# Products and sums of the modulation vectors on GpSimd, interleaved in pairs, with the column as a per-partition scalar

## What is computed

```python
def adaln(cond, mod_w, mod_b):
    m = jax.nn.silu(cond) @ mod_w + mod_b        # mod_w: 1024 x 6144, one per layer
    return jnp.split(m, 6, axis=-1)

x = first_block(x, ...)                          # two layers, does not use m
...
sh1, sc1, g1, sh2, sc2, g2 = adaln(c, mod_w[i], mod_b[i])          # i = 0, 1
csh1, csc1, ... = adaln(c_ctx, mod_w[i], mod_b[i])                 # layer 0 only
a = rms_norm_2(h_lat, norm1_g[i]) * (1 + sc1) + sh1
```

## Time and profile before

| | before |
|---|---|
| median of three runs | 1936.33 us |
| profiled execution, span | 1938.2 us |
| PE busy | 1887.5 us (97%) |
| DVE busy | 784.5 us (40%) |
| ACT busy | 546.1 us (28%) |
| POOL busy | 734.9 us (38%), nearly all of it before 990 us |
| mean granted TensorE clock | 0.996 |

### The profile page before, as it was taken

How to read it: one execution, slowest core, us unless ns; L and a number is a source line. 1 busy time by engine, 2 the same in 40 slices (tenths; PEclk the granted TensorE clock), 3 DMA queues, 4 the chain that set the end, 5 groups by cost and what they waited for, 6 DMA issues and landing times.

```text
span 1938.2 us, 26187 instructions
## 1 busy us (share of the span) xinstructions
PE 1887.5 (97%) x9836; PEld 1008.9 (52%) x9836; DVE 784.5 (40%) x1672; ACT 546.1 (28%) x1187; POOL 734.9 (38%) x1065
## 2 busy tenths in 40 slices
PE   9999999999999999999999999999999999998998
PEld 6544556566546555565655456664543444444433
DVE  1445453433220344453346463753542411234533
ACT  3133433122421234421225231651311221012110
POOL 1767667765766667667630012100110100001111
PEclk9999999999999999999999999999999999999999
DMA  7323343334335243342332422313799822056997
GB/s 293 118 90 112 122 141 120 114 139 149 140 114 188 106 164 128 117 155 99 137 135 90 171 82 87 120 52 166 263 388 382 309 98 87 5 212 236 371 371 278
DMA packets 70300, 322.17 MB, mean 166 GB/s; under 512 B 8680, under 2 KB 11174, under 8 KB 55590
## 3 DMA queue, kind: packets, MB, share of 16 engines
q1 hardware_dynamic: 41688, 216.22, 29.7%
q0 software_dynamic: 25328, 92.81, 14.0%
q10 hardware_dynamic: 3168, 11.54, 1.5%
HBM read 287.51 MB, written 33.03 MB: 165 GB/s over the span
## 4 chain that ended last, share of the span: by engine, by line
PE 85%; DVE 5%; DMA 5%; issue 2%; ACT 1%; DVEq 1%; SPq 0%; POOL 0%; ACTq 0%; POOLq 0%
PE psA L462 23%; PE psA L1854 10%; PE psA L454 9%; PE psA L2001 6%; PE psA L1895 6%; PE psA L627 6%; PE psSO L2020 4%; PE psT L441 3%; PE psA L503 3%; PE psSO L532 3%; DMA pool_mem<-in_w_v 2%; PE psSO L542 2%; DMA pool_mem<-in_w_gu 1%; DVE pool_mem L2951 1%; PE psT L1970 1%
## 5 line engine op out<-in xcount | busy, mean ns | idle before, releaser
L462 PE MATMUL psA<-gB,pool_mem 128*128 128x512 f32 x1024 | 455.3, 597 | 0.0
L397 POOL TENSOR_TENSOR pool_mem<-pool_mem,cs 128x256 f32<-128x256 f32 x448 | 272.8, 641 | 136.0 <-DMA pool_mem<-in_mod_w 135.4
L462 PEld LDWEIGHTS psA<-gB,pool_mem 128*128 128x128 f32 x1024 | 189.5, 190 | 224.2 <-issue 224.2
L401 POOL TENSOR_TENSOR pool_mem<-pool_mem 128x256 f32<-128x256 f32 x336 | 248.1, 766 | 34.6 <-issue 26.6
L1854 PE MATMUL psA<-pool_mem 128*128 128x512 f32 (+1 forms) x528 | 209.0, 554 | 1.9 <-DVE pool_mem L1615 1.1
L454 PE MATMUL psA<-pool_mem,gB 128*128 128x256 f32 (+2 forms) x768 | 189.8, 403 | 2.7 <-ACT gB L796 1.2
L1803 POOL DMA_INDIRECT pool_mem<-xs_scratch,idx x38 | 35.5, 935 | 387.9 <-DVE idx L2625 359.5
L454 PEld LDWEIGHTS psA<-pool_mem,gB 128*128 128x128 f32 x768 | 143.8, 190 | 45.4 <-issue 6.2
L1854 PEld LDWEIGHTS psA<-pool_mem 128*128 128x128 f32 x528 | 99.2, 190 | 105.1 <-issue 99.8
L2001 PE MATMUL psA<-pool_mem 128*32 128x512 f32 (+1 forms) x896 | 141.1, 593 | 0.0
L1895 PE MATMUL psA<-pool_mem 128*128 128x512 f32 x256 | 113.9, 595 | 0.8 <-issue 0.8
(11 more groups left out here) (357 smaller groups left out, 2412.3 us busy)
## 6 DMA issues: line engine op xcount, KB each, us to landing
pool_mem<-in_w_gu SPq DMA_DIRECT2D x32, 2048.0 KB, 9.2
pool_mem<-in_mod_w POOLq DMA_DIRECT2D x56, 1024.0 KB, 7.9
pool_mem<-in_w_dn SPq DMA_DIRECT2D x32, 1024.0 KB, 13.8
pool_mem<-in_w_qk SPq DMA_DIRECT2D x24, 1024.0 KB, 4.9
ys_scratch<-pool_mem ACTq DMA_DIRECT2D x22, 512.0 KB, 10.1
pool_mem<-in_odd_w_in SPq DMA_DIRECT2D x5, 2048.0 KB, 9.7
pool_mem<-in_w_out SPq DMA_DIRECT2D x4, 2048.0 KB, 8.1
macc_scratch<-pool_mem POOLq DMA_DIRECT2D x56, 128.0 KB, 2.1
```

The lines of the kernel that those rows point to most:

```text
L397: nc.gpsimd.tensor_tensor(wm[:, b, k], wm[:, b, k], c_all[:, k].to_broadcast([P, MCH]), ALU.mult)
L401: nc.gpsimd.tensor_tensor(wm[:, b, k], wm[:, b, k], wm[:, b, n + k], ALU.add)
L462: m = nc.tensor.matmul(psA[:, n % 2, :], w(i), src[:, k, :], start=(i == 0), stop=(i == len(ks) - 1))
```

## The change

The 8 products, 7 sums and their operands stay the same in number. Seven of the eight products read the column of `cs` as a per-partition scalar instead of as a broadcast tensor; the product of slice 0 keeps the old form. The order is now: two products (slices k and 4 + k), a drain, their sum, a drain, four times; then the two sums, a drain, the last sum, a drain. A call of `multiply` has 10 drains instead of 4. Loads, stores, waits and all other engines are untouched.

```diff
             def multiply(b, row, loaded):
                 pool.wait_ge(m_loaded[b], loaded)
-                c_all = cs[:, row * KD:(row + 1) * KD].rearrange("p (k o) -> p k o", o=1)
-                for k in range(KD):
-                    nc.gpsimd.tensor_tensor(wm[:, b, k], wm[:, b, k], c_all[:, k].to_broadcast([P, MCH]), ALU.mult)
+                def times(k):
+                    if k == 0:
+                        c_0 = cs[:, row * KD:row * KD + 1]
+                        nc.gpsimd.tensor_tensor(wm[:, b, 0], wm[:, b, 0], c_0.to_broadcast([P, MCH]), ALU.mult)
+                        return
+                    nc.gpsimd.tensor_scalar(wm[:, b, k], wm[:, b, k], cs[:, row * KD + k:row * KD + k + 1], None, ALU.mult)
+
+                def plus(k, n, out):
+                    nc.gpsimd.tensor_tensor(out, wm[:, b, k], wm[:, b, n + k], ALU.add)
+
+                for k in range(4):
+                    times(k)
+                    times(4 + k)
+                    pool.drain()
+                    plus(k, 4, wm[:, b, k])
+                    pool.drain()
+                for k in range(2):
+                    plus(k, 2, wm[:, b, k])
                 pool.drain()
-                for n in (4, 2):
-                    for k in range(n):
-                        nc.gpsimd.tensor_tensor(wm[:, b, k], wm[:, b, k], wm[:, b, n + k], ALU.add)
-                    pool.drain()
-                nc.gpsimd.tensor_tensor(macc[:, b], wm[:, b, 0], wm[:, b, 1], ALU.add)
+                plus(0, 1, macc[:, b])
                 pool.drain()
```

## The result

The changed kernel takes 2137.84 us (median of 5 runs, 2135.53 to 2141.04) against 1936.33 us (5 runs, 1931.9 to 1937.83): a ratio of 1.1057, 95% interval 1.1031 to 1.1083. It is 201.5 us slower, where 1930.0 us and at the most 1953 us were predicted. The profiled execution spans 2136.3 us, 198.1 us more than the one before.

What follows compares the result with a forecast made beforehand. TensorE, busy 97% of the span, was taken to bound the kernel. From the 1938.2 us span, 7.2 us of removed blocks gave 1931.0 us; the run offset made it 1930.0 us, range 1926 to 1953 us, likeliest case 1926 to 1934.

Steps and rivals of the forecast that it cites:

- The two ways: GpSimd can move the time only through TensorE's few idle microseconds or by missing a date on which someone waits.
- the date: When SP, waiting for GpSimd's last store, must load the sums for DVE's `fold_columns`: 1029.9 us, about 40 us of slack.
- The runs are broken: GpSimd runs of at most two instructions end four full DVE blocks; 7.2 us gained, bounds 3.9 and 8.7 us.
- The 1.5 us set aside for smaller blocks: Allowance for DVE additions still held briefly: 0.7 us in the stretch of L1046, 0.8 us at two later places.
- Rival C: DVE blocks last one GpSimd instruction or return in small pieces elsewhere: 1936 us, between 1933 and 1939; chance 0.24.
- its last step: Result of the sum: 1931.0 us from the profiled span, 1929.1 us if all runs measure 1.9 us less; 1930.0 us taken.
- Seven products take a scalar: A GpSimd product by a per-partition scalar takes 0.40 us at 256 columns, range 0.29 to 0.61 us.
- Six more drains: Gaps in a GpSimd call: four of 0.24 us (or 0.42) before sums, five of 0.15 us between sums.
- The sum of a call: A `multiply` call takes 10.0 us, no change; with 0.1 us allowed, +6 us over 56 calls, GpSimd ending near 995 us.
- What the slack allows: With TensorE 7 us earlier, 33 us or 0.59 us a call; date missed from a scalar product of 0.48 us on.
- Rival B: GpSimd late at DVE's `fold_columns` wait, from scalar products over 0.48 us or larger gaps: 1946 to 1977 us; chance 0.24.

Runs made afterwards that it cites:

- shifted: Kernel before the change, with one memset and one product ahead of GpSimd's first load, runs of eight products unbroken: 1936.0 us, ratio 1.001.
- the two split kernels: Kernel before the change, drains added inside the second buffer's products: one after the fourth, 1929.89 us (0.9977); or after the third and sixth, 1928.14 us (0.9978).
- before_again: Kernel before the change, unchanged, profiled a second time: 1930.15 us (1 run), span 1928.6 us.
- sum_drains: Kernel before the change, with a drain after each of the six sums, four more drains per call: 1936.37 us (1 run).
- order_only: Changed kernel with its new order and ten drains, but all eight products in the old broadcast form: 2014.51 us, ratio 1.0408 to the kernel before.

## Why the prediction was wrong, step by step

**What bounds the kernel: right.** The two ways were named, and the time went through both: 14.5 us gained in the small gaps and behind them, 209.1 us lost at the date.

**The runs are broken: the mechanism right, one price left out, and some luck.** 7.2 us were expected, 8.6 us of idle time went, and TensorE was 14.5 us earlier. The sum priced a block at TensorE's wait alone. The piece of slow clock behind it, 4.6 us in all, stood in the prediction's own rows: two matmuls of L676 take 2.07 us behind the long wait and five take 2.41 us in layer 1. The luck is in the comparison: the first profile met four blocks, and other executions met one or none with their runs of eight unbroken. DVE's longest instruction of L1046 is 1.05 us now (678/683/1054 ns), and TensorE waits 0.45 us before L676's successor instead of 5.75 us. Timelines of DVE and PE in the changed kernel:
```profile
88.86 2.89 DVE L1057 TENSOR_TENSOR pool_mem<-pool_mem 32x512 f32<-32x512 f32 x4
...
93.12 2.41 PE L687 MATMUL psA<-pool_mem 128*128 128x512 f32 x5 [0.45 <-DVE pool_mem L1039]
```
The 1.5 us set aside for smaller blocks was nearly unused. Rival C, that a block is one instruction long whatever stands behind it, is refuted by the lengths in shifted and the two split kernels together. Its other half, that the gain is a matter of phase, is not refuted for this one profile. The rule of the Trainium skill that went with it ("SBUF — State Buffer", section "Who interferes with whom", a lock for the length of an instruction) fits the changed kernel's rows, where blocks are short, but not the 5.30, 3.07 and 2.48 us above. That the first kernel's profile overstated its usual idle time, which the prediction allowed for in its last step, is what before_again shows.

**Seven products take a scalar: the first of the two terms that failed.** It was put at 0.40 us with 0.29 and 0.61 as bounds; it is 0.92 us. Two reasons were given. "It reads one tensor less, so I see no reason for more" was no row but a guess, and it made the upper bound. The other, a fixed part plus half the slope for one input, predicts the copy to the nanosecond (0.400 us at 256 columns) and misses this instruction, whose slope is three times the copy's: reading one input is not what sets its cost per column. The error is 7 x 0.52 x 56 = 204 us of GpSimd time against the sum, and 7 x (0.92 - 0.61) x 56 = 122 us beyond the bound. The Trainium skill, "GPSIMD Engine Reference", gave two prices: about line rate for one input (section 4.1 "Engine selection"), which here holds for the copy alone, and 1.8 cycles per element (section 3.1 "Elementwise — side-by-side cycle accounting"), by which I had estimated 0.57 us. Both are under the 0.922 us that the rows show, and the measurement decides.

**Six more drains: the second term that failed.** The gaps between later steps are 0.142, 0.147 and 0.170 us, near the 0.15 us read from the earlier trace rows and under the 0.24 us that three of them were given. But the sum took the first one at 0.24 to 0.42 us, as "the gap that a drain leaves". It is the time until the engine's own transfers have landed, and it showed short in the earlier trace rows because eight products covered it. In the first buffer it is 1.63 us in the median and 2.37 us in the mean now. The trace of before has the 2.54 us that contradicts my reading; I had looked at one call and its neighbour, where it is 0.42 and 0.24 us, and not at the largest gap of its kind. The mechanism needed to be asked for: the drain was moved from behind eight products to behind two, and what it waits for did not move.

**The sum of a call.** 10.0 us were predicted for both buffers. Measured, from first product to end of last sum: 15.97 us in the first buffer and 14.07 us in the second (before: 11.05 and 10.54 us, means over the kernel; the call that I read took 10.23 us, less than the mean). The two calls and the loads between them make 8.6 us more a pair (42.56 us against 33.94), 241 us in 28 pairs, against the 235.8 us at SP.

**What the slack allows: the mechanism right, the date 4 to 7 us too late.** 1024 us was worked out (1029.9 + 1 - 7), and 1017 to 1020 us is measured. The way from SP's load to TensorE was nearly right. It takes 1233.92 - 1226.74 = 7.2 us in the changed kernel, so the date in the profile before would have been 1039.3 - 7.2 = 1032.1 us, where the prediction has 1031. The memset and the 16 copies of `fold_columns` are not on that way: they end at 1230.41 us, and DVE then waits 1.17 us for the piece to land. What was too small is the 7 us by which TensorE comes earlier. It comes 14.5 us earlier, and 1032.1 - 14.5 = 1017.6 us, the date of the changed kernel. With the right date the limit would have been (10.05 + 27/56 - 7.3) / 7 = 0.46 us instead of 0.48 us, so this miss decided nothing.

**Rival B was the case, and was underpriced.** Its place (DVE's wait in `fold_columns`) and its two causes (a product over 0.48 us, gaps larger than 0.24 us) are what happened, both at once. It ended at 1977 us because each cause had been bounded, and the bounds had been taken one at a time. With the measured sizes the same sum, over the spans, gives 1938.2 - 14.5 + (235.8 - 26.7) + 3.4 = 2136.2 us, with 26.7 us of slack (1017.6 - 990.9) and the 3.4 us that the kernel is slower behind the stall; the profiled execution spans 2136.3 us.

## What to carry to other kernels

Before an instruction on GpSimd is replaced by another form, time both at the width that is used: fewer operands did not mean less time, and the form with a per-partition scalar took 1.5 times the form with a broadcast column. Before a drain is moved ahead, ask what the engine has in flight at its new place, stores included; look for the largest gap behind that drain in the old trace, not for a typical one. And price an engine off the critical path by its date: 27 us of slack spread over 56 calls is 0.5 us a call, which is what one of the seven products was misjudged by. Before a gain is read off one profile, take a second of the same kernel: here two profiles of one kernel differ by 5.6 us of idle TensorE and by 9.6 us of span.

## What the runs showed of the hardware

A drain on GpSimd ends when the engine's own loads and stores under way have landed, also those that the next instruction doesn't touch. The next instruction starts 0.28 us after a load's landing (28 of 28 pairs of the changed kernel, 0.23 us in one of them) and 0.17 to 0.18 us after a store's (27 of 28 pairs of order_only). With nothing in flight a drain between later steps leaves a gap of 0.14 to 0.17 us and costs 0.18 us with the overlap that is lost (sum_drains, order_only).

GpSimd's elementwise instructions differ by a factor of 2.3 at 256 columns of f32: copy 0.40, product by a broadcast column 0.61, sum of two tensors 0.73, product by a constant 0.85, product by a scalar from memory 0.92 us.

A DVE instruction that starts between 0.2 us before and 0.1 us after the first of a run of GpSimd products can be held until the run ends, not for one instruction: 4.7 to 5.3 us for eight products, 2.4 to 3.1 us for four, 2.2 to 2.5 us for three. All 24 such blocks are beside a run that starts right behind the issue of a store on GpSimd. Not every instruction in that window is held. How many such meetings an execution has varies from run to run of the same kernel (one and four in two profiles), and with them its time. What in the two engines does this, no run here shows.

Behind an idle TensorE the granted clock stays low for a while, and that is part of the price of a wait: 0.50 in the stretches of 6.8 and 3.5 us at waits of 5.75 and 2.49 us (before), and for 4.7 us after the stall of 209 us (changed kernel).
